# Second feed-forward on a residual divided by the norm's root, the final norm taking the root back in

## The chip, the cores and the metric

The kernel runs on one core of a Trainium2 chip. The metric is device microseconds (us) of one execution; the kernel before takes 1284.77 us, the median of 3 runs (1284.58 to 1285.41). Engines are named as in the profile: PE is TensorE (PEld its weight loads), DVE VectorE, ACT ScalarE, POOL GpSimd, SP SyncE. A name such as L736 is a line of the kernel's file.

## What is computed

One layer of a decoder trunk for 576 tokens (512 of a prompt and 64 of decode requests), 1024 wide: a first feed-forward, a mixer, a cross attention, a second feed-forward, and a last norm. Only its end matters here:

```python
h = h + cross_attend(rms_norm(h, g_cross), ...)
g, u = split(rms_norm(h, g_ffn2) @ w_ffn2_gu)      # 2816 columns each
h = h + 0.5 * (silu(g) * u) @ w_ffn2_down
y = rms_norm(h, g_final)        # x * rsqrt(mean(x*x) + EPS) * gain, per token
```

With R = rsqrt(mean(h*h) + EPS) of a token, g and u are the products of the weights with h times gain, each times that token's R.

## The kernel before

Tokens lie along the free dimension (576 columns, in two halves of 288), features on the 128 partitions; `h` is 8 chunks of 128x576. Every fp32 product is made of three reduced-precision (fp32r) matmuls: high by high, high by low, low by high. So each weight block has a high part (a rounding copy on ACT) and a low part (the difference, on DVE or POOL), and so have the activations.

Each engine has its own program, written out by hand in the order in which it runs; only semaphores tie the engines together. A wait holds back everything behind it on that engine. SP loads the weight blocks into `raw`, four buffers in turn.

The second feed-forward (from 877 to 1270 us) has three groups of columns: 8, 8 and 6 tiles of 128. A tile has a gate block and an up block. In the first group one tile is done plainly (`dense`, 48 matmuls for a block); the other 21 tiles are "units", in which gate and up of both token halves are four 2x2 block products done in seven (Strassen-Winograd): A11, A12, S1, S2, S4, A22, S3, with 12 matmuls each. After each group comes a down group: 8 blocks, each added to a chunk of `h`. Below, F is the first unit of the second feed-forward; F+1 to F+6 follow in the same group.

What each engine does for a unit v:

- PE, `unit(v)`: waits for the low part of A11 (`lo_a`, from POOL) and, in the first unit, until the plain gate is out of PSUM (`ps_free`); then the seven products. S2 of a unit waits until ACT has copied A11's product out (`e_ok`), S4 until ACT has copied S1's out.
- ACT, `unit(v)`: `high_last` (high parts of S3 and A22, L1562 and L1564), the copies out of PSUM (`keep`, L1583), the next unit's high parts (L1544, L1552), the gate's SiLU (L1602), and the high part of the hidden tile (L1607).
- DVE, `unit(v)`: the sums of weights for the next unit (L2118, L2121, L2125, L2128), low parts (L2134, L2139), `finish(v - 1)`, the low part of the hidden tile (L2179), and the gate's sum (L2206) and its product with R (L2208).
- `finish` makes the up tile `us` from two PSUM products (L2168), multiplies it by R (L2170) and by the SiLU (L2172). ACT's second copy out of PSUM in the next unit waits for L2168.
- POOL, `plain_lows`: for each unit the low part of A11 and A12 (L676) and of A22 (L679). Around it POOL adds the squares of `h` for the norms (`sums`, L519).

At the start of the second feed-forward ACT takes the logarithm and exponential of the mean square, and DVE refines R with one Newton step (`rms(3)`, L2069 to L2071). Then DVE evicts the plain gate (L2213), makes the low parts of F's sums (L2134) and one more sum (L2125), evicts the plain up block times R (L2217), and multiplies it by the SiLU (L2220).

At the end POOL has summed seven of eight chunks of squares in `acc`, PE makes the token means from `acc` and the last chunk, ACT takes the root (L1999), DVE inverts it (`inverse`, a reciprocal and a Newton step), and the transposed rows times gain are scaled by it on DVE and ACT and stored.

Of the kernel before, what the change touches and what calls it, by code (L numbers as in the profile page):

```python
# [9 lines left out]
ALU = mybir.AluOpType  # L10
ACT = mybir.ActivationFunctionType
# [4 lines left out]
KD = D // P  # L16
TP, NB, BT = 512, 8, 8
TS = NB * BT
T = TP + TS
TH = T // 2  # L20
NT = (T + P - 1) // P
# [3 lines left out]
EPS = 1e-6  # L25
# [26 lines left out]
def hymba_kernel(nc, A, O, consts):  # L52

    with ExitStack() as ctx:
# [10 lines left out]
        def S(name):  # L65
            if name not in sems:
                sems[name] = ctx.enter_context(nc.semaphore(name))
            return sems[name]


        cst = sb("cst", [P, C_END])
# [7 lines left out]
        eps = sb("eps", [P, 1])  # L79
# [22 lines left out]
        def view(base, at, *dims):  # L102
            n = 1
            for d in dims:
                n *= d
            v = base[:, at:at + n]
            if len(dims) == 1:
                return v
            names = "abcd"[:len(dims)]
            return v.rearrange(f"p ({' '.join(names)}) -> p {' '.join(names)}",  # L110
                               **{k: d for k, d in zip(names[1:], dims[1:])})
# [121 lines left out]
        def operand(v, j, low):  # L233

            if j >= A22:
                return (xl if low else xh)[:, 0:HK, TH + P * (j - A22):TH + P * (j - A22 + 1)]
            return view(ARr, 16 * T + 1024 * (5 * (v % 2) + j) + 512 * low, HK, P)

        def operands(v, j, n, low):

            return view(ARr, 16 * T + 1024 * (5 * (v % 2) + j), n, 1024)[:, :, 512 * low:512 * low + 512]

        yy = PR[:, 0:8, :]
        YB = (4, 6, 0, 2, 4)
# [256 lines left out]
        def _(e):  # L501
            e.memset(mean_d[:], 1.0 / D).then_inc(s_const, 1)
            e.memset(eps[:], EPS).then_inc(s_const, 1)
            e.memset(one[:], 1.0).then_inc(s_const, 1)
            e.memset(acc[:, T:], 0.0).then_inc(s_const, 1)
            e.memset(mst[:], 1.0).then_inc(s_const, 1)

            def sums(m):

                if m > 1:  # L510
                    e.wait_ge(acc_ready, 8 * (m - 1))
                e.wait_ge(ss, m)
                e.memset(acc[:, 0:T], 0.0).then_inc(acc_zero, 1)
                e.wait_ge(acc_zero, m)
                for k in range(KD - 1 if m == 4 else KD):
                    e.wait_ge(sq_ready, 8 * (m - 1) + k + 1)
                    if 8 * (m - 1) + k:
                        e.wait_ge(acc_ready, 8 * (m - 1) + k)
                    e.tensor_tensor(acc[:, 0:T], acc[:, 0:T], sq[:, k % 2, :], ALU.add).then_inc(acc_ready, 1)  # L519
# [117 lines left out]
            def s5_tables():  # L637
# [30 lines left out]
                        double()  # L668
                e.sem_inc(S("pool_points"), 1)

            def plain_lows(i):

                for v in range(FIRST_UNIT[i], FIRST_UNIT[i + 1]):
                    n = units[v]
                    e.wait_ge(S("hi_ok"), 4 * v + 1)
                    TTT(operands(v, A11, 2, 1), raw[:, n % 4, :].rearrange("p (s x) -> p s x", s=2),  # L676
                        operands(v, A11, 2, 0).bitcast(F32), ALU.subtract).then_inc(S("lo_a"), 1)
                    e.wait_ge(S("hi_ok"), 4 * v + 4)
                    TTT(operand(v, A22, 1), raw[:, (n + 1) % 4, 512:1024].rearrange("p (k n) -> p k n", k=HK),  # L679
                        operand(v, A22, 0).bitcast(F32), ALU.subtract).then_inc(S("lo_a"), 1)  # L680

            plain_lows(0)
            s5_chain()
# [40 lines left out]
            e.wait_ge(S("s_mm"), 4)  # L724
            e.memset(PTz, 0.0).then_inc(S("pool_points"), 1)
            sums(3)
            for i in range(2, 5):
                plain_lows(i)
            sums(4)
# [760 lines left out]
        def _(e):  # L1490
# [505 lines left out]
            for i in range(2, 5):  # L1996
                seven_group(i)
            e.wait_ge(ss, 5)
            e.activation(yst[:, 0, :], bank(1, NT), ACT.Sqrt, bias=eps[:]).then_inc(rt, 1)  # L1999
            e.wait_ge(S("yst_ok"), 1)  # L2000
            for m, j in enumerate(LEAVE):
                w = min(P, T - j * P)
# [7 lines left out]
        def _(e):  # L2010
# [3 lines left out]
            def own(ins):  # L2014
                mark(ins, "dve_own")
# [33 lines left out]
            def halves(b):  # L2049
                return PS[:, b:b + 2, 0:TH]  # L2050

            def two(ap):
                return ap.rearrange("p (a t) -> p a t", a=2)
# [6 lines left out]
                    STT(chunk(xl, k), chunk(h, k), gains[:, gain_of[m], bass.ds(k, 1)], chunk(xh, k).bitcast(F32),  # L2060
                        ALU.mult, ALU.subtract).then_inc(x_lo, 1)

            def inverse(root, square, tmp, name):

                own(e.reciprocal(root, root))
                newton(root, square, tmp, name)

            def newton(root, square, tmp, name):
                own(STT(tmp, root, -0.5, root, ALU.mult, ALU.mult))  # L2069
                own(STT(tmp, square, EPS, tmp, ALU.add, ALU.mult))  # L2070
                mark(STT(root, tmp, 1.5, root, ALU.add, ALU.mult), name)  # L2071

            def rms(m):
                if m == 0:
                    e.wait_ge(S("xsq_ok"), NT)
                    own(TSC(row_means, mst[:, 0:NT], 1.0 / D, None, ALU.mult))
                    e.wait_ge(rt, 1)
                    inverse(roots, row_means, row_tmp, "dve_own")
                    for j in range(NT):
                        w = min(P, T - j * P)  # L2080
                        TSC(xdiag[0:w, j * P:j * P + w], ident[0:w, 0:w], roots[0:w, j:j + 1], float(D), ALU.mult, ALU.mult).then_inc(S("xdiag_ok"), 1)
                    e.wait_ge(ss, 1)
                    mark(CP(R[:], bank(4, T)), "r_ready")
                    return
                if m == 3:
                    for j in (S1, S2, S4):
                        sum_of(j, FIRST_FFN2)
                e.wait_ge(rt, m + 1)
                newton(R[:], us[:] if m == 3 else bank(4, T), gs[:], "r_ready")

            def down(g):
                def body(i, n, par):
# [71 lines left out]
            def finish(v):  # L2164

                e.wait_ge(S("pr_done"), 7 * v + 7)
                e.wait_ge(S("e_ok"), 4 * v + 4)
                TTT(two(us[:]), two(sq[:, 1, :]), bank(u_bank(v), TH)[:, None, :].broadcast_to([P, 2, TH]), ALU.subtract).then_inc(S("c_ok"), 1)  # L2168
                e.wait_ge(S("c_ok"), 2 * v + 2)
                own(TTT(us[:], us[:], R[:], ALU.mult))  # L2170
                e.wait_ge(g_act, before(v) + 1)
                TTT(us[:], us[:], act[:], ALU.mult).then_inc(hid, 1)  # L2172

# [36 lines left out]
            def hidden(i, n, par, g):  # L2210

                if par == 0:
                    TTT(two(gs[:]), halves(6 if n == 2 else 0), two(R[:]), ALU.mult).then_inc(g_scaled, 1)  # L2213
                    e.wait_ge(g_scaled, i + (g["f0"] + 1))
                    e.sem_inc(ps_free, 1)
                else:
                    TTT(two(us[:]), halves(2), two(R[:]), ALU.mult).then_inc(ps_free, 1)  # L2217
                    e.wait_ge(ps_free, seq(n) + 3)
                    e.wait_ge(g_act, i + (g["f0"] + 1))
                    TTT(us[:], us[:], act[:], ALU.mult).then_inc(hid, 1)  # L2220
# [14 lines left out]
            def seven_group(i, within=None):  # L2235

                for v in range(FIRST_UNIT[i], FIRST_UNIT[i + 1]):
                    unit(v)
                finish(v)
                hidden_low(v)  # L2240
                g = groups[groups.index(seven_groups[i]) + 1]
                for b in range(KD):
                    n = g["n0"] + b
                    e.wait_ge(mm_done, seq(n) + 3)
                    STT(two(h[:, b, :]), halves(2 * (b % 2)), 0.5, two(h[:, b, :]), ALU.mult, ALU.add).then_inc(ps_free, 1)
                    if n == len(blocks) - 1:
                        e.wait_ge(ps_free, seq(n) + 3)
                        TSC(yy[:, b, :], h[:, b, :], gains[:, G_FINAL, b:b + 1], None, ALU.mult).then_inc(S("yy_v"), 1)
                    if b < KD - 2 or i in (1, 4):
                        conv(n + 2)  # L2250
                    if i in (0, 2, 3):
                        if b == KD - 3:
                            for j in (S1, S2, S3, S4):
                                sum_of(j, v + 1)
                        elif b == KD - 2:
                            low_sums(v + 1)
                    if i == 1 and b == 2:
                        second_half_low()
                    if within and b == 4:
                        within()  # L2260
                    elif within and b > 4:
                        matrix_step(2 * b - 10)
                        matrix_step(2 * b - 9)
# [509 lines left out]
            for i in range(2, 5):  # L2773
                seven_group(i)
            e.wait_ge(rt, 5)
            inverse(yst[:, 0, :], bank(1, NT), yst[:, 1, :], "yst_ok")
            for m, j in enumerate(LEAVE):
                w = min(P, T - j * P)
                e.wait_ge(S("y_tr"), m + 1)
# [48 lines left out]
```

## Time and profile before

| | before |
|---|---|
| time, median of 3 runs | 1284.77 us |
| span of the profiled execution (first to last instruction) | 1282.0 us |
| busy: PE, DVE, ACT, POOL | 1261.7, 857.1, 531.3, 353.9 us |
| granted TensorE clock, mean | 0.998 |
| the chain that ended last, on PE | 92% |

The profiled execution has no total of its own beside its span; the median of the timed runs is 2.77 us longer than that span, which is what lies around the first and the last instruction. A row of a timeline gives start, duration, engine, line, operation and operands, and in brackets the idle time of the engine before it and what ended that. Two matmuls that follow each other freely overlap in such rows, since the duration includes the drain of the pipeline.

### The profile page before, as it was taken

To read this page: it belongs to the slowest core of one execution; us is meant where nothing else is said; L and a number is where in the kernel's file an instruction comes from. 1 tells how busy PE (TensorE), PEld (TensorE's weight loads), DVE (VectorE), ACT (ScalarE), POOL (GpSimd) and SP (SyncE) were. 2 spreads that over 40 slices of the span, in tenths; PEclk is the share of its full clock that TensorE was granted. 3 is DMA by queue.
4 is the path that set the end of the run, shared out by engine and by line. 5 is a ranking of instruction groups with operands and counts; after the bars stand their busy time and mean duration, and the time that the engine had idled before them with its cause. 6 is when DMAs were issued, how large, how long until landed. Compare 5 with 4: busy or idle time off the path is not lost.

```text
span 1282.0 us, 24086 instructions
## 1 busy us (share of the span) xinstructions
PE 1261.7 (98%) x10151; PEld 1218.5 (95%) x10151; DVE 857.1 (67%) x1061; ACT 531.3 (41%) x803; POOL 353.9 (28%) x411
## 2 busy tenths in 40 slices
PE   7999999999999999999999999999999999999997
PEld 6999999999999999999899997599999999999997
DVE  4986479847885636558565437479995589637953
ACT  6644145511224422574443324246553255414543
POOL 0026723288893201000002100032330133102321
PEclk9999999999999999999999999999999999999999
DMA  6233323263223442125333756322332323323322
GB/s 182 81 96 90 91 85 99 83 137 91 74 65 94 91 81 65 51 69 154 119 89 93 232 197 223 122 83 66 100 99 83 99 83 99 91 83 91 87 63 74
DMA packets 221084, 129.94 MB, mean 101 GB/s; under 512 B 22256, under 2 KB 213280, under 8 KB 220960
## 3 DMA queue, kind: packets, MB, share of 16 engines
q1 hardware_dynamic: 217024, 123.83, 33.8%
q10 hardware_dynamic: 3952, 4.58, 1.1%
q8 instruction: 80, 1.31, 0.4%
q14 instruction: 28, 0.23, 0.1%
HBM read 121.42 MB, written 5.78 MB: 99 GB/s over the span
## 4 chain that ended last, share of the span: by engine, by line
PE 92%; DVE 4%; ACT 2%; issue 1%; DMA 1%; SPq 0%; ACTq 0%; DVEq 0%
PE PS L736 89%; PE PS L1361 1%; DMA AR<-in_x_prompt 1%; PE PS L806 0%; ACT wh L1500 0%; ACT gua L1649 0%; DVE Hs L2452 0%; DVE xl L2139 0%; PE PS L1338 0%; DVE AR L2780 0%; PE PS L953 0%; PE PS L1447 0%; DVE ARr L2134 0%; DVE yl L2233 0%; DVE wl L2027 0%
## 5 line engine op out<-in xcount | busy, mean ns | idle before, releaser
L1500 ACT ACTIVATE wh<-raw 128x1024 fp32r<-128x1024 f32 (+1 forms) x126 | 130.1, 1032 | 373.7 <-PE PS L736 373.1
L736 PE MATMUL PS<-yh,wh 128*128 128x288 f32 x960 | 205.6, 296 | 0.0
L736 PE MATMUL PS<-yl,wh 128*128 128x288 f32 x960 | 204.7, 295 | 0.0
L736 PE MATMUL PS<-yh,wl 128*128 128x288 f32 x960 | 204.6, 295 | 0.0
L2027 DVE TENSOR_TENSOR wl<-raw,wh 128x1024 fp32r<-128x1024 f32 (+1 forms) x126 | 154.9, 1229 | 63.7 <-ACT wh L1500 62.3
L736 PE MATMUL PS<-xh,ARr 128*128 128x288 f32 x792 | 174.1, 297 | 0.4 <-ACT sq L1583 0.2
L736 PE MATMUL PS<-xh,wh 128*128 128x288 f32 x736 | 164.4, 305 | 0.1
L736 PE MATMUL PS<-xh,wl 128*128 128x288 f32 x736 | 158.1, 297 | 0.0
L736 PE MATMUL PS<-xl,wh 128*128 128x288 f32 x736 | 157.9, 296 | 0.0
L736 PEld LDWEIGHTS PS<-yh,wh 128*128 128x128 f32 x960 | 154.1, 189 | 1.5 <-DVE yl L2705 0.8
L736 PEld LDWEIGHTS PS<-yh,wl 128*128 128x128 f32 x960 | 154.3, 189 | 0.0
L736 PEld LDWEIGHTS PS<-yl,wh 128*128 128x128 f32 x960 | 154.3, 189 | 0.0
L676 POOL TENSOR_TENSOR ARr<-raw,ARr 128x1024 fp32r<-128x1024 f32 x33 | 85.1, 2578 | 179.6 <-ACT ARr L1544 179.2
L736 PEld LDWEIGHTS PS<-xh,ARr 128*128 128x128 f32 x792 | 132.4, 188 | 1.1 <-ACT sq L1583 0.7
L519 POOL TENSOR_TENSOR acc<-acc,sq 128x576 f32<-128x576 f32 x31 | 52.6, 1697 | 276.9 <-issue 163.8
L736 PEld LDWEIGHTS PS<-xh,wh 128*128 128x128 f32 x736 | 118.3, 190 | 2.6 <-issue 1.1
L736 PEld LDWEIGHTS PS<-xh,wl 128*128 128x128 f32 x736 | 119.0, 190 | 0.0
L736 PEld LDWEIGHTS PS<-xl,wh 128*128 128x128 f32 x736 | 118.8, 190 | 0.0
L736 PE MATMUL PS<-xl,ARr 128*128 128x288 f32 x396 | 117.2, 296 | 0.0
L736 PE MATMUL PS<-ARr 128*128 128x288 f32 x792 | 114.5, 294 | 1.4 <-ACT sq L1583 1.4
L736 PEld LDWEIGHTS PS<-ARr 128*128 128x128 f32 x792 | 107.9, 188 | 1.6 <-issue 1.6
L1583 ACT ACTIVATE sq<-PS 128x288 f32<-128x288 f32 x132 | 54.1, 410 | 131.2 <-PE PS L736 83.3
(378 smaller groups left out, 2183.5 us busy)
## 6 DMA issues: line engine op xcount, KB each, us to landing
raw<-in_w_ffn_gu SPq DMA_DIRECT2D x88, 512.0 KB, 3.9
raw<-in_w_ffn_down SPq DMA_DIRECT2D x32, 512.0 KB, 3.9
raw<-in_w_in SPq DMA_DIRECT2D x16, 512.0 KB, 4.0
raw<-in_w_ckv SPq DMA_DIRECT2D x16, 512.0 KB, 3.8
raw<-in_w_ffn_down SPq DMA_DIRECT2D x16, 384.0 KB, 3.4
Hs<-in_cache_mem_k SPq DMA_DIRECT2D x6, 1024.0 KB, 6.5
raw<-in_w_out SPq DMA_DIRECT2D x8, 512.0 KB, 4.0
raw<-in_w_cq SPq DMA_DIRECT2D x8, 512.0 KB, 4.3
```

Source lines behind the costliest of these rows:

```text
L519: e.tensor_tensor(acc[:, 0:T], acc[:, 0:T], sq[:, k % 2, :], ALU.add).then_inc(acc_ready, 1)
L676: TTT(operands(v, A11, 2, 1), raw[:, n % 4, :].rearrange("p (s x) -> p s x", s=2), operands(v, A11, 2, 0).bitcast(F32), ALU.subtract).then ...
L736: return e.matmul(out, lhsT, rhs, start=start, stop=stop, **kw)
L1361: last = e.transpose(bank(4 + q % 3, P, at=f * M + j * P), KB[b][:, j, at:at + P], ident)
L1500: e.activation(wh[:, n % 2, 0:K * P], raw[:, n % 4, 0:K * P], ACT.Copy).then_inc(w_hi, 1)
L1583: e.activation(out, bank(b, TH), ACT.Copy, **kw).then_inc(S("e_ok"), 1)
L2027: TTT(wl[:, n % 2, 0:K * P], raw[:, n % 4, 0:K * P], wh[:, n % 2, 0:K * P].bitcast(F32), ALU.subtract).then_inc(w_lo, 1)
```

## The change

`h` is divided by R before the second feed-forward adds to it, so that the up tiles need not be multiplied by R: (h + 0.5 W(silu(g) u R)) / R = h/R + 0.5 W(silu(g) u). The gates still are multiplied. 1/R is (mean + EPS) times R; it is made by one more DVE operation in `rms(3)` and lies in `rinv`, in a constant's place that is free by then. POOL multiplies the eight chunks of `h` by it, between the low parts of the first group's units. The final norm of the new residual needs EPS/R^2 in the place of EPS: POOL starts the sum of squares with KD * EPS * rinv * rinv in the place of zero, and the last root and its Newton step add no EPS.

```diff
+        rinv = view(cst, C_SCAN, T)
...
-            e.memset(acc[:, T:], 0.0).then_inc(s_const, 1)
+            e.memset(acc[:, T:], 1.0).then_inc(s_const, 1)
...  POOL, sums(m)
-                e.memset(acc[:, 0:T], 0.0).then_inc(acc_zero, 1)
+                if m == 4:
+                    mul(acc[:, 0:T], rinv, rinv)
+                    e.tensor_scalar(acc[:, 0:T], acc[:, 0:T], KD * EPS, None, ALU.mult).then_inc(acc_zero, 1)
+                else:
+                    e.memset(acc[:, 0:T], 0.0).then_inc(acc_zero, 1)
...  POOL
+            def unscaled(k):
+                TTT(h[:, k, :], h[:, k, :], rinv, ALU.mult).then_inc(S("g_ok"), 1)
...  POOL, plain_lows(i), at the end of each unit v
+                    if i == 2:
+                        unscaled(v - FIRST_FFN2)
+                        if v == FIRST_FFN2 + 3:
+                            unscaled(KD - 1)
...  POOL, main order
             sums(3)
+            e.wait_ge(x_hi, 8 * 4)
+            e.wait_ge(x_lo, 8 * 4)
+            e.wait_ge(S("xg_ok"), 2 * HK)
+            e.wait_ge(S("t_sum"), 8 * HK)
+            e.wait_ge(S("rinv_ok"), 1)
             for i in range(2, 5):
                 plain_lows(i)
...  ACT, the last root
-            e.activation(yst[:, 0, :], bank(1, NT), ACT.Sqrt, bias=eps[:]).then_inc(rt, 1)
+            e.activation(yst[:, 0, :], bank(1, NT), ACT.Sqrt).then_inc(rt, 1)
...  DVE, rms(m)
                 newton(R[:], us[:] if m == 3 else bank(4, T), gs[:], "r_ready")
+                if m == 3:
+                    mark(STT(rinv, us[:], EPS, R[:], ALU.add, ALU.mult), "rinv_ok")
...  DVE, finish(v)
-                own(TTT(us[:], us[:], R[:], ALU.mult))
+                if v < FIRST_FFN2:
+                    own(TTT(us[:], us[:], R[:], ALU.mult))
...  DVE, hidden(): the plain up block
+                elif g is groups[FFN2]:
+                    e.wait_ge(g_act, i + (g["f0"] + 1))
+                    TTT(two(us[:]), halves(2), two(act[:]), ALU.mult).then_inc(hid, 1)
+                    e.wait_ge(hid, i + (g["f0"] + 1))
+                    e.sem_inc(ps_free, 1)
...  DVE, seven_group(i), before the down group
+                if i == 2:
+                    e.wait_ge(S("g_ok"), KD)
...  DVE, the last inverse
-            inverse(yst[:, 0, :], bank(1, NT), yst[:, 1, :], "yst_ok")
+            inverse(yst[:, 0, :], bank(1, NT), yst[:, 1, :], "yst_ok", 0.0)
```

## Rows read from the trace of the kernel before

**Rows 1.** The page: busy us of each engine, share of the span, instructions.
```profile
PE 1261.7 (98%) x10151; PEld 1218.5 (95%) x10151; DVE 857.1 (67%) x1061; ACT 531.3 (41%) x803; POOL 353.9 (28%) x411
```

**Rows 2.** Windows: stretch, length, busy us per engine, granted clock, DMA share, GB/s.
```profile
895.00:900.00 5.00, 3.62 (x28) 3.41 (x27) 4.93 (x7) 4.42 (x7) 2.56 (x2) 1.00 0.38 109
...
940.00:960.00 20.00, 20.00 (x153) 20.00 (x152) 18.96 (x22) 11.21 (x19) 8.23 (x4) 1.00 0.38 107
```

**Rows 3.** The chain that ended last, 855 to 935 us: start, length, what.
```profile
891.40 5.03 PE PS L736 x36
...
897.36 0.31 ACT sq L1583
...
910.46 0.42 ACT sq L1583
```

**Rows 4.** Timeline of PE, the first two units of the second feed-forward.
```profile
897.80 1.82 PE L736 MATMUL PS<-ARr 128*128 128x288 f32 x12 [1.38 <-ACT sq L1583]
...
905.82 1.74 PE L736 MATMUL PS<-ARr 128*128 128x288 f32 x12
907.40 0.30 PE L736 MATMUL PS<-xh,ARr 128*128 128x288 f32 x1
...
910.93 0.40 PE L736 MATMUL PS<-xh,ARr 128*128 128x288 f32 x1 [0.18 <-ACT sq L1583]
```

**Rows 5.** Waits, 1225 to 1240 us: who waited for whom, us, times, longest.
```profile
PEld PS L736 <- DVE yl L2179: 0.3, 1, 0.3
```

**Rows 6.** Timeline of DVE, from the last token sums to the second unit.
```profile
876.03 0.51 DVE L2159 SCALAR_TENSOR_TENSOR AR<-h,gains,AR 128x288 f32<-128x288 f32 x1
...
884.08 1.00 DVE L2159 SCALAR_TENSOR_TENSOR AR<-h,gains,AR 128x288 f32<-128x288 f32 x1
...
889.70 0.76 DVE L2071 SCALAR_TENSOR_TENSOR R<-gua,R 128x576 f32<-128x576 f32 x1
890.49 0.76 DVE L2213 TENSOR_TENSOR gua<-PS,R 128x576 f32<-128x576 f32 x1
...
898.83 2.80 DVE L2139 TENSOR_TENSOR xl<-AR,xh 128x512 fp32r<-128x512 f32 x1
...
904.72 0.76 DVE L2208 TENSOR_TENSOR gua<-gua,R 128x576 f32<-128x576 f32 x1
...
910.47 1.57 DVE L2170 TENSOR_TENSOR gua<-gua,R 128x576 f32<-128x576 f32 x1
```

**Rows 7.** Timeline of POOL, around the start of the second feed-forward.
```profile
880.47 1.43 POOL L519 TENSOR_TENSOR acc<-acc,sq 128x576 f32<-128x576 f32 x1 [4.98 <-ACT sq L1526]
881.86 2.91 POOL L676 TENSOR_TENSOR ARr<-raw,ARr 128x1024 fp32r<-128x1024 f32 x1
...
898.69 2.40 POOL L676 TENSOR_TENSOR ARr<-raw,ARr 128x1024 fp32r<-128x1024 f32 x1
907.32 1.30 POOL L679 TENSOR_TENSOR xl<-raw,xh 128x512 fp32r<-128x512 f32 x1 [6.23 <-ACT xh L1564]
```

**Rows 8.** Groups by line and form, DVE, 910 to 1235 us: busy, mean ns.
```profile
L2170 DVE TENSOR_TENSOR gua<-gua,R 128x576 f32<-128x576 f32 x21 | 28.5, 1357 | 0.7
...
L2139 DVE TENSOR_TENSOR xl<-AR,xh 128x512 fp32r<-128x512 f32 x19 | 13.2, 692 | 14.6 <-ACT xh L1562 14.6
```

**Rows 9.** Timeline of ACT, the third unit.
```profile
921.61 0.41 ACT L1583 ACTIVATE sq<-PS 128x288 f32<-128x288 f32 x1 [1.98 <-DVE gua L2168]
```

**Rows 10.** Timeline of DVE, evictions of the first and the second down group.
```profile
978.01 0.76 DVE L2245 SCALAR_TENSOR_TENSOR h<-PS,h 128x576 f32<-128x576 f32 x1 [2.32 <-PE PS L736]
...
984.25 0.76 DVE L2245 SCALAR_TENSOR_TENSOR h<-PS,h 128x576 f32<-128x576 f32 x1 [3.86 <-PE PS L736]
...
1117.10 0.76 DVE L2245 SCALAR_TENSOR_TENSOR h<-PS,h 128x576 f32<-128x576 f32 x1 [2.47 <-PE PS L736]
...
1123.50 0.76 DVE L2245 SCALAR_TENSOR_TENSOR h<-PS,h 128x576 f32<-128x576 f32 x1 [4.02 <-PE PS L736]
```

**Rows 11.** Timeline of POOL, before the last down group's squares.
```profile
1235.33 1.56 POOL L519 TENSOR_TENSOR acc<-acc,sq 128x576 f32<-128x576 f32 x1 [14.52 <-issue]
```

More of the change, by code:

```diff
@@ L2061, in norm_in, with inverse, newton @@
                         ALU.mult, ALU.subtract).then_inc(x_lo, 1)
-            def inverse(root, square, tmp, name):
+            def inverse(root, square, tmp, name, bias=EPS):
                 own(e.reciprocal(root, root))
-                newton(root, square, tmp, name)
-            def newton(root, square, tmp, name):
+                newton(root, square, tmp, name, bias)
+            def newton(root, square, tmp, name, bias=EPS):
                 own(STT(tmp, root, -0.5, root, ALU.mult, ALU.mult))
-                own(STT(tmp, square, EPS, tmp, ALU.add, ALU.mult))
+                own(STT(tmp, square, bias, tmp, ALU.add, ALU.mult))
                 mark(STT(root, tmp, 1.5, root, ALU.add, ALU.mult), name)
```

## The prediction, made before the change was run

> **What bounds the kernel now.** I read the page's busy times first: PE is busy 98% of the span, DVE 67%, POOL 28% [rows 1]. The change takes work from DVE, so the next question is where PE waits for DVE. Windows of the second feed-forward answer it for most of the stretch: between 940 and 960 us PE is busy for all 20.00 us although DVE is busy for 18.96 [rows 2]. DVE is nearly full there and still no bound. The chain of waits then shows where PE does stand still. From 891.40 us it runs three products (36 matmuls) of the first unit, F; ACT copies a product out from 897.36 to 897.67; PE goes on at 897.80 [rows 3, 4]. The timeline of PE calls that 1.38 us of idle time, and 0.18 us at 910.93, again behind ACT's copy [rows 4]. The third place is the entry to the last down group, 0.3 us behind the low part of the last hidden tile [rows 5]. The chain names no other PE stall between 911 us and the tail. So whatever DVE saves can return about 2 us here; the rest must fall into time in which DVE waits.
>
> True lost time is a little more than the idle time, because freely following products overlap: one that began at 905.82 and is listed with 1.74 us was followed at 907.40, not 907.56 [rows 4]. With 0.16 us added the first stall is 1.54 and the second 0.34 us. A product of 12 matmuls takes 1.6 us from start to start.
>
> **The change part by part.**
>
> *Twenty-one multiplications by R leave DVE.* L2170 is 28.5 us over 21 units, mean 1.36, but 0.76 where nothing holds it up [rows 8] (an operation of that shape, L2208, takes 0.76 [rows 6]). In the units they lie beside a PE that does not wait; I cost them at nothing, except at two places. At the second unit the copy that PE waits for does not depend on L2170, so nothing there. At the last down group it stands in the chain that PE waits for (difference, times R, times SiLU, high part, low part): taking 0.76 us out of a chain that is 0.3 us late removes the stall: -0.3 us. What is late next is the PE itself.
>
> *The plain up block* is evicted and multiplied by the SiLU in one operation instead of two: -0.79 on DVE with its gap. Its release of PSUM now waits for the SiLU, which ACT does while DVE makes two other operations (L2134, L2125) between gate and up block: nothing.
>
> *1/R is one more DVE operation* before the gate's eviction: +0.79 (as L2071, 0.76 and a gap [rows 6]). Together with the line above DVE's queue behind them is where it was.
>
> *POOL's low part of unit F moves behind 1/R.* This is the term that decides. Before, POOL did it as soon as the squares were added, from 881.86 on [rows 7], long before PE wanted it at 891.40. Now five waits stand ahead of `plain_lows(2)`, and the last of them is 1/R. Four are over earlier: the x parts and the token sums all come out ahead of R on DVE's queue. Two steps give the time. First, DVE is a little earlier: L2159 took 1.00 us instead of 0.51 while POOL's 2.91 us operation ran [rows 6, 7], and with that operation gone 0.49 us come back. R is then ready at 889.70 + 0.76 - 0.49 = 889.97 and 1/R at 890.76. Second, POOL starts 0.15 us later (PE began 0.15 us after the gate's eviction at 890.49 + 0.76 ended), takes 2.40 us where nothing blocks it [rows 7], and PE starts 0.15 us after that, at 893.45 instead of 891.40: +2.05 us. Everything queued on PE is behind that wait. Three products later S2 could start at 893.45 + 4.80 = 898.25. Before it started at 897.80, held by the copy that is now at the same place (DVE's queue to it neither grew nor shrank, or is up to 0.49 earlier). So the new wait swallows the old stall and adds 0.45 us. If DVE is not earlier (+0.49) and POOL's operation takes its blocked length of 2.91 (+0.51), it adds 1.45. The lower end is a POOL that costs nothing and a stall that goes by DVE's 0.49: -0.5.
>
> *POOL multiplies eight chunks by 1/R* in units F to F+6 (two in F+3). The nearest row is the addition of the same shape, 1.43 us [rows 7]; I take it. POOL has the room: 8.23 of 20 us in the steady stretch [rows 2], 1.43 more for each unit of 11.2 (84 matmuls). But POOL and DVE get into each other's way: L2139 took 2.80 us instead of 0.69 while POOL's operation of 898.69 to 901.09 ran, L2170 1.57 [rows 6 to 8]. The Trainium skill, page "SBUF — State Buffer", section "SBUF: two separate sides", makes this a lock on a shared port pair, held for a whole instruction by whichever started first, against DVE operations with two SBUF inputs. The trace agrees: L2139 ended 0.54 us after POOL's operation did.
>
> In unit F this is on the path. DVE's chain to the second stall is L2139, L2125, L2134, the gate's sum and L2208 (ending 905.48), then ACT's SiLU, and so on to the copy at 910.46 [rows 3, 6]. L2139 now meets the tail of the first scaling instead of the whole low part: 0.9 us less. L2125 behind it, free before, can meet the next unit's low part: up to 2.2 more. With 0.49 earlier from above that is between -1.4 and +0.8 us; S4 of F+1 could start, by PE alone, at 910.93 - 0.34 + 0.45 = 911.04, +0.11. So the end of this stretch moves by +0.11 to +0.8, and I take +0.5, as POOL will have been waiting when L2139 lets go. This replaces the +0.45 and is not added to it; with the upper end of the POOL wait it is +1.1 to +1.5.
>
> From F+2 on the margin is thin: the copy that S4 waits for ended at 922.02 [rows 9], and PE wanted it at 910.93 plus 84 matmuls of 0.133, 922.1. But PE is now 0.5 later and DVE has 1.57 less to do in each unit, against at most one scaling (1.43) to wait for. I cost this at nothing; the case in which it fails is the first rival. In F+3 POOL does 1.30 [rows 7] + 2 x 1.43 + 2.40 us and some blocked time, some 8 us, and the low part that it ends with is wanted about as late: nothing, or 0.3.
>
> *The wait of DVE for all eight scalings* stands before the first down eviction (978.01 [rows 10]); the last scaling comes at the head of F+6, most of a unit and a block of 6.24 us earlier: nothing.
>
> *POOL's new start of the sum* replaces one clearing by two operations; the first addition is at 1235.33, and POOL is idle for 14.52 us ahead of it [rows 11]. Two operations of even 2.40 us each fit: nothing on the path. The last root and Newton step have the same operations with other constants: nothing.
>
> The sum: +0.5 (start, both stalls included) - 0.3 (last group) = +0.2 us on a span of 1282.0, so 1282.2; the median is 2.77 us above the profiled span, and the forecast is 1285.0. Bounds of these terms: -0.5 - 0.34 - 0.3 = -1.1 below, +1.5 + 0.3 above: 1283.6 to 1286.6. What a measurement of this kernel can tell from no change is about 0.2%, 2.57 us; all of this is within.
>
> **The rivals.**
>
> 1. *POOL's scalings hold DVE up in each unit* (slower). Place: the units F+1 to F+6, whose copy had 0.1 us of margin. In a unit DVE's operations with two SBUF inputs can meet 5.1 us of POOL work (1.30 + 1.43 + 2.40) instead of 3.7. Decisive point: when the added waits exceed the 1.57 us that L2170 gave back and the 0.6 us of margin. If L2172 waits for a scaling (1.43) and L2179 or L2208 for the low part (2.40), the excess is 3.83 - 2.17, up to 1.7 us a unit, 10 us in six; at a third of that, 3.3 us, 1288.3. For it: the long L2139. Against: the removed operation was itself the one that met POOL. Chance 0.16.
>
> 2. *The matmuls fall into another rhythm.* The first down group's blocks follow each other every 6.24 us, the second's every 6.40 with the same DVE operations beside them [rows 10]: 48 matmuls at 130 or 133 ns. I know no cause. A moved start may change it: a group of eight blocks is worth 1.28 us, the last (six steps of weights) 0.96. If the first loses it, 1286.3; if the second and third gain it, 1282.8. Chance 0.15, both signs. The same skill page, section "Who interferes with whom", says that PE never waits on another engine's SBUF traffic. By that rule a lighter DVE cannot speed the matmuls; the two rhythms beside equal DVE work agree with it.
>
> 3. *The late POOL start costs nothing and the stalls shrink* (the lower bound): 1.1 us less than before, 1283.6. For it: DVE's 0.49. Against: 2.40 us of POOL cannot fit between 890.76 and 891.40. Chance 0.10.
>
> 4. *The units are bound by DVE after all*, and 0.76 us or more come back in each of 18 units: about -14, 1271. For it: 18.96 of 20 us busy. Against: PE has no gap there. Chance 0.04.
>
> **How the numbers follow.** Forecast 0.55, the rivals 0.16, 0.15, 0.10, 0.04. Faster by over 0.2% (below 1282.2): the last rival and 0.04 of the second at its low end, 0.08. Slower (above 1287.3): 0.13 of the first rival, and 0.05 for sums of the upper bound and a lost rhythm: 0.18. Same: 0.74. The range takes the forecast's bounds, and of the rhythms and the lock as much as leaves out 2 in 10: 1283.2 to 1287.4.
>
> **What would show it.** PE's first product of F starts near 893.4 instead of 891.40, released by POOL; no stall is left before S2 of F; a stall of a few tenths stays before S4 of F+1, and none in F+2 to F+6; PE's wait at the last down group is gone; DVE is about 28 us less busy and POOL about 14 more, with no other place that changes. PE stalls that repeat in each of F+1 to F+6 would make the prediction wrong on one side, a PE that is quicker in the units on the other.

## The result: 1287.8 us, 0.24% slower

| | before | after |
|---|---|---|
| time, median of 20 runs each | 1284.9 us | 1287.8 us (1286.04 to 1291.05) |
| ratio after to before, 95% interval | | 1.0024 (1.0019 to 1.0030) |
| span of the profiled execution | 1282.0 us | 1285.8 us |

1.0024 of 1284.9 is 3.1 us more (2.4 to 3.9). The forecast was 1285.0 with an upper end of 1287.4, so the time lies outside the range, on the side of rival 1.

Lines move with the edits. The matmul L736 is L755 now, POOL's low parts L676 and L679 are L686 and L689, DVE's `finish` is L2189 (difference) and L2194 (times SiLU). New are L679 (POOL's scaling of a chunk) and L2110 (1/R). The page's busy times of the kernel after, to be held against [rows 1]:

```profile
PE 1264.7 (98%) x10151; PEld 1220.5 (95%) x10151; DVE 851.3 (66%) x1040; ACT 531.3 (41%) x803; POOL 368.1 (29%) x420
```

POOL has 14.2 us more, as forecast. DVE has 5.8 us less, not 28: the first sign that something replaced what was removed. It is seen in DVE's groups by line and form, 910 to 1235 us before and 910 to 1238 us after (busy, mean ns). Before, first the operation that went and then the one behind it; after, the one that is left:

```profile
L2170 DVE TENSOR_TENSOR gua<-gua,R 128x576 f32<-128x576 f32 x21 | 28.5, 1357 | 0.7
L2172 DVE TENSOR_TENSOR gua<-gua 128x576 f32<-128x576 f32 x21 | 15.9, 758 | 0.7
```

```profile
L2194 DVE TENSOR_TENSOR gua<-gua 128x576 f32<-128x576 f32 x21 | 35.5, 1692 | 0.7
```

28.5 us of multiplications by R are gone, and 19.6 of them are back in the multiplication behind them. It takes 1.69 us now instead of 0.76. The first operation of `finish` with two SBUF inputs meets POOL's low part, whichever operation that is.

Where PE stands still is in its timeline (in brackets the idle time and its releaser; against [rows 4]):

```profile
894.29 0.40 PE L755 MATMUL PS<-xh,ARr 128*128 128x288 f32 x1 [2.15 <-POOL ARr L686]
912.67 0.40 PE L755 MATMUL PS<-xh,ARr 128*128 128x288 f32 x1 [0.62 <-ACT sq L1602]
924.39 0.40 PE L755 MATMUL PS<-xh,ARr 128*128 128x288 f32 x1 [0.30 <-ACT sq L1602]
...
936.12 0.40 PE L755 MATMUL PS<-xh,ARr 128*128 128x288 f32 x1 [0.33 <-ACT sq L1602]
959.15 0.40 PE L755 MATMUL PS<-xh,ARr 128*128 128x288 f32 x1 [0.32 <-ACT sq L1602]
...
970.87 0.40 PE L755 MATMUL PS<-xh,ARr 128*128 128x288 f32 x1 [0.32 <-ACT sq L1602]
```

The first row is the forecast wait for POOL, and S2 of F has no row of its own any more. 912.67 is S4 of F+1. The other four are S4 of F+2, F+3, F+5 and F+6, which did not wait before. From 912.67 to 924.39 and on to 936.12 are 11.72 and 11.73 us, where 84 matmuls of 0.133 need 11.17.

A bracket shows less than is lost, since matmuls that follow freely overlap. Below, "lost" is the sum of the start-to-start times of successive matmuls above 0.133 us, in three places:

| lost, us | F to S4 of F+1 | F+2 to F+6 | last down group | sum |
|---|---|---|---|---|
| before | 2.42 | 0 | 0.30 | 2.72 |
| after | 3.30 | 2.52 | 0 | 5.82 |

The difference is 3.1 us, the whole of the measured one. Of the 2.52, four units have 0.57 to 0.60 each and F+4 has 0.18. DVE and POOL show where they come from. First the kernel before in unit F+1, DVE and then POOL:

```profile
909.69 0.74 DVE L2168 TENSOR_TENSOR gua<-sq,PS 128x576 f32<-128x576 f32 x1
910.47 1.57 DVE L2170 TENSOR_TENSOR gua<-gua,R 128x576 f32<-128x576 f32 x1
912.07 0.76 DVE L2172 TENSOR_TENSOR gua<-gua 128x576 f32<-128x576 f32 x1
```

```profile
907.32 1.30 POOL L679 TENSOR_TENSOR xl<-raw,xh 128x512 fp32r<-128x512 f32 x1 [6.23 <-ACT xh L1564]
908.58 2.84 POOL L676 TENSOR_TENSOR ARr<-raw,ARr 128x1024 fp32r<-128x1024 f32 x1
```

Then the kernel after at the same place:

```profile
911.44 0.74 DVE L2189 TENSOR_TENSOR gua<-sq,PS 128x576 f32<-128x576 f32 x1
912.21 2.94 DVE L2194 TENSOR_TENSOR gua<-gua 128x576 f32<-128x576 f32 x1
```

```profile
909.06 1.30 POOL L689 TENSOR_TENSOR xl<-raw,xh 128x512 fp32r<-128x512 f32 x1 [5.51 <-ACT xh L1583]
910.32 1.87 POOL L679 TENSOR_TENSOR h<-h,cst 128x576 f32<-128x576 f32 x1
912.16 2.38 POOL L686 TENSOR_TENSOR ARr<-raw,ARr 128x1024 fp32r<-128x1024 f32 x1
```

Before, POOL's low part ended at 911.42; L2170 arrived 0.95 us ahead of that and ended 0.62 after it. From its start to the end of L2172 is 2.36 us. After, the scaling stands ahead of the low part. It ends as L2189 ends, POOL goes straight on, and L2194 arrives 0.05 us too late: it waits for the whole low part (912.16 + 2.38 = 914.54) and ends 0.61 us behind it. Its 2.94 us are 0.58 more than the two operations of before took together, and the loop over DVE, ACT's copy and PE had no slack, so PE loses those 0.58 in each such unit. Both chains start from ACT's high parts of the same unit, so the near miss repeats: L2194 takes 2.94 to 2.96 us in F+1, F+2, F+4 and F+5, and PE loses 0.57 to 0.60 us in the unit behind each. In F+3 two scalings stand ahead of the low part (3.27 us, up to 937.03), and L2194, arriving at 935.65, waits for the second of them instead: 1.99 us, and PE loses 0.18 in F+4.

The profiled spans differ by 3.8 us, not 3.1. The rest lies in code that the change doesn't touch (last section). Wherever a run's time and span are both known, the time is 1.75 to 1.86 us longer (1287.58 and 1285.8 for this profile). So, as an estimate, the profiled execution of before took 1283.8 us, about 1 us less than its median, and the 2.77 us of the section on time and profile before are not all outside the instructions.

### The profile page after: what moved, and what is told of

It reads as the page before. It is cut to its first block, busy times and chain, and to the rows that moved or that the text cites. A ratio compares the mean times of both kernels' runs of the same rounds, so it can differ in the third digit from the quotient of the medians.

```text
span 1285.8 us, 24079 instructions
## 1 busy us (share of the span) xinstructions
PE 1264.7 (98%) x10151; PEld 1220.5 (95%) x10151; DVE 851.3 (66%) x1040; ACT 531.3 (41%) x803; POOL 368.1 (29%) x420
## 4 chain that ended last, share of the span: by engine, by line
PE 89%; DVE 6%; issue 2%; ACT 2%; DMA 1%; SPq 0%; DVEq 0%; ACTq 0%
PE PS L755 85%; PE PS L1380 1%; DVE gua L2194 1%; DMA AR<-in_x_prompt 1%; ACT wh L1519 0%; DVE xl L2160 0%; DVE PS L2149 0%; DVE ARr L2155 0%; PE PS L1466 0%; PE PS L825 0%; DVE PS L2142 0%; DVE PS L2139 0%; ACT gua L1668 0%; DVE gua L2189 0%; DVE Hs L2481 0%
## 5 line engine op out<-in xcount | busy, mean ns | idle before, releaser
L755 PE MATMUL PS<-yh,wh 128*128 128x288 f32 x960 | 205.9, 296 | 0.0
L755 PE MATMUL PS<-yl,wh 128*128 128x288 f32 x960 | 205.0, 295 | 0.0
L755 PE MATMUL PS<-yh,wl 128*128 128x288 f32 x960 | 205.0, 295 | 0.0
L755 PE MATMUL PS<-xh,ARr 128*128 128x288 f32 x792 | 174.6, 297 | 4.1 <-POOL ARr L686 2.1
L755 PE MATMUL PS<-xh,wh 128*128 128x288 f32 x736 | 164.4, 305 | 0.1
L755 PE MATMUL PS<-xh,wl 128*128 128x288 f32 x736 | 157.8, 296 | 0.0
L755 PE MATMUL PS<-xl,wh 128*128 128x288 f32 x736 | 157.7, 296 | 0.0
L755 PEld LDWEIGHTS PS<-yh,wh 128*128 128x128 f32 x960 | 154.1, 188 | 1.3 <-DVE yl L2734 0.8
L755 PEld LDWEIGHTS PS<-yh,wl 128*128 128x128 f32 x960 | 154.4, 188 | 0.0
L755 PEld LDWEIGHTS PS<-yl,wh 128*128 128x128 f32 x960 | 154.4, 188 | 0.0
L755 PEld LDWEIGHTS PS<-xh,ARr 128*128 128x128 f32 x792 | 132.2, 188 | 5.9 <-ACT sq L1602 3.4
L686 POOL TENSOR_TENSOR ARr<-raw,ARr 128x1024 fp32r<-128x1024 f32 x33 | 82.4, 2496 | 189.1 <-ACT ARr L1563 179.7
L755 PEld LDWEIGHTS PS<-xh,wh 128*128 128x128 f32 x736 | 118.1, 190 | 2.6 <-issue 1.1
L755 PEld LDWEIGHTS PS<-xl,wh 128*128 128x128 f32 x736 | 118.8, 189 | 0.0
L755 PEld LDWEIGHTS PS<-xh,wl 128*128 128x128 f32 x736 | 118.7, 189 | 0.0
L755 PE MATMUL PS<-xl,ARr 128*128 128x288 f32 x396 | 117.0, 296 | 0.0
L755 PE MATMUL PS<-ARr 128*128 128x288 f32 x792 | 114.2, 294 | 0.0
L2274 DVE SCALAR_TENSOR_TENSOR h<-PS,h 128x576 f32<-128x576 f32 x40 | 30.2, 756 | 118.3 <-PE PS L755 118.3
```

Of the source, the lines that this page charges most:

```text
L755: return e.matmul(out, lhsT, rhs, start=start, stop=stop, **kw)
```

## The experiments

Theory A: the place of the scaling in POOL's order makes DVE wait a whole low part. Theory B: the late start of POOL (the wait for 1/R) sets a rhythm that makes the units late. Theory C: 1.43 us more of POOL's work costs this anywhere in the unit. "Lost" is as above; before it is 2.42, 0 and 0.30.

**no_scaling.** After, without POOL's eight scalings (so the residual is not divided and y is not the layer's):

```diff
-                    if i == 2:
-                        unscaled(v - FIRST_FFN2)
-                        if v == FIRST_FFN2 + 3:
-                            unscaled(KD - 1)
+                    if i == 2 and v == FIRST_FFN2:
+                        e.sem_inc(S("g_ok"), KD)
```

> The changed kernel without POOL's eight multiplications of h by 1/R; the residual is then not divided, so the outputs y are not the reference's; all else, the late start of POOL's first low part too, stays. Theory A (port lock): the up product L2194 meets POOL's low part only because a scaling stands ahead of that; without the scalings L2194 takes under 1.7 us in the units, PE has no stall of 0.3 us or more in the units F+2 to F+6, and the time is that of the kernel before within 0.5 us (start +0.44, second unit's stall at most +0.1, last down group -0.30). Theory B (late start): PE begins unit F 2 us late, DVE and ACT fall out of step with it and stay so; the stalls of 0.5 us in F+2 to F+6 remain and the time stays about 3 us above before.

1285.74 us, ratio 1.0006 (0.9998 to 1.0015); lost 3.93, 0, 0. The late start is still there (PE idle for 2.15 us behind POOL), and the stalls of the units are gone: B falls. DVE (here L2192 is the multiplication by the SiLU) and POOL in F+1:

```profile
909.57 0.74 DVE L2187 TENSOR_TENSOR gua<-sq,PS 128x576 f32<-128x576 f32 x1
910.34 1.67 DVE L2192 TENSOR_TENSOR gua<-gua 128x576 f32<-128x576 f32 x1
```

```profile
907.20 1.29 POOL L689 TENSOR_TENSOR xl<-raw,xh 128x512 fp32r<-128x512 f32 x1 [6.86 <-ACT xh L1581]
908.99 2.40 POOL L686 TENSOR_TENSOR ARr<-raw,ARr 128x1024 fp32r<-128x1024 f32 x1 [0.50 <-ACT ARr L1561]
```

The low part ends at 911.39 and DVE waits only for its rest, as L2170 did before. Of the 3.93 some 1.5 us are TensorE's clock (last section), not a wait. PE was late by that too, which could hide stalls here; scale_between, below, has the same late start at full clock and loses 0.17 us in F+2 to F+6.

**early_low.** The five waits stand behind the low parts of F and ahead of the first scaling, so POOL's first low part comes early again:

```diff
+                    if v == FIRST_FFN2:
+                        ready_to_scale()
...
             sums(3)
-            e.wait_ge(x_hi, 8 * 4)
...
-            e.wait_ge(S("rinv_ok"), 1)
```

> The changed kernel with the five waits moved from ahead of POOL's first low part of unit F to ahead of the first scaling, so that this low part is made early, as before the change. Theory A: PE starts unit F within 0.6 us of the gate's release again, S2 of F waits 1 to 1.5 us as before the change, but the stalls of about 0.57 us in F+1 to F+6 stay: 2 to 3 us above before. Theory B: with the late start gone the units run without stalls: 0 to 0.5 us below before.

1289.01 us, ratio 1.0032 (1.0021 to 1.0043); lost 3.79, 2.51, 0. POOL's low part of F starts at 884.11 and PE no longer waits for it, yet the entry loses no less: PE now waits 0.9 us at F for the gate's eviction (L2240), which stands behind 1/R (L2115) on DVE, 0.82 at S2 and 1.15 at S4 of F+1. DVE, and PE's first product of F, 0.15 us behind the end of that eviction:

```profile
892.74 0.76 DVE L2115 SCALAR_TENSOR_TENSOR cst<-gua,R 128x576 f32<-128x576 f32 x1
893.53 0.76 DVE L2240 TENSOR_TENSOR gua<-PS,R 128x576 f32<-128x576 f32 x1
```

```profile
894.44 0.37 PE L760 MATMUL PS<-xh,ARr 128*128 128x288 f32 x1 [0.91 <-issue]
```

The units lose what they lost. So taking the late start away saves nothing, neither at the entry nor behind it. The time is further above before than the 2 to 3 us expected, since PE loses more at the entry than was thought.

**scale_between.** The scaling goes between the low part of A11 and A12 and that of A22, the other side of the long operation; POOL does the same work:

```diff
+                    if i == 2 and v > FIRST_FFN2:
+                        unscaled(v - FIRST_FFN2 - 1)
                     e.wait_ge(S("hi_ok"), 4 * v + 4)
...              (low part of A22)
-                    if i == 2:
-                        unscaled(v - FIRST_FFN2)
...
+                    if i == 2 and v == FIRST_FFN2 + 6:
+                        unscaled(KD - 2)
+                        unscaled(KD - 1)
```

> The changed kernel with each scaling moved from behind the low part of A22 to ahead of it, where POOL is idle for 6 us in every unit (units F+1 to F+6; the last two scalings follow the last unit's low part). POOL does as much work as in the change. Theory A: it is the place in POOL's order that costs: L2194 under 1.7 us, no stalls of 0.3 us or more in F+2 to F+6, time within 0.6 us of before. Theory B: as long as the start is late the stalls stay, about 3 us above before. A third possibility, that POOL's added work costs wherever it stands: stalls of 0.3 us or more move to other DVE operations, 2 to 3 us above before.

1286.49 us, ratio 1.0006 (0.9997 to 1.0014); lost 3.31, 0.17, 0. This tells A from C: eight scalings in the same units, and the stalls are gone. DVE and POOL in F+1:

```profile
912.63 0.74 DVE L2190 TENSOR_TENSOR gua<-sq,PS 128x576 f32<-128x576 f32 x1
913.41 1.55 DVE L2195 TENSOR_TENSOR gua<-gua 128x576 f32<-128x576 f32 x1
```

```profile
910.26 1.30 POOL L691 TENSOR_TENSOR xl<-raw,xh 128x512 fp32r<-128x512 f32 x1 [5.51 <-ACT xh L1584]
911.51 2.83 POOL L686 TENSOR_TENSOR ARr<-raw,ARr 128x1024 fp32r<-128x1024 f32 x1
914.30 1.95 POOL L679 TENSOR_TENSOR h<-h,cst 128x576 f32<-128x576 f32 x1
```

The low part follows the A22 one at once, as before; DVE waits for its last 0.93 us, and then the scaling waits for DVE (1.95 us instead of 1.43), where nobody waits for it.

**idle_scaling.** The kernel before with a multiplication of the same shape on POOL at the change's places (its product is read by nobody); as in the change, DVE waits for all eight before the down group:

```diff
+                    if i == 2:
+                        if v == FIRST_FFN2:
+                            e.wait_ge(r_ready, 4)
+                        idle_scaling(v - FIRST_FFN2)
+                        if v == FIRST_FFN2 + 3:
+                            idle_scaling(KD - 1)
```

> The kernel before with one part of the change alone: POOL multiplies the chunks of h by R into a place that nothing reads, at the very points where the change scales h, with the two multiplications in F+3; DVE keeps L2170, POOL's first low part stays early. Theory A: now L2170 meets POOL's whole low part (2.9 us instead of 1.58), DVE's loop grows by about 1.3 us in each unit and PE waits about 1.2 us in each of four to six units: 5 to 7 us above before, twice what the change costs, since there L2170's own 0.76 us are saved. Theory B: nothing, within 0.5 us of before, as the start is not late.

1293.37 us, ratio 1.0063 (1.0050 to 1.0076), 8.1 us more; lost 3.54, 5.93, 0.30. The added work costs without the rest of the change, and more than with it. The expectation had the size nearly right and the wrong operation. DVE and POOL in F+1:

```profile
912.87 0.76 DVE L2180 TENSOR_TENSOR gua<-gua,R 128x576 f32<-128x576 f32 x1
913.66 2.84 DVE L2182 TENSOR_TENSOR gua<-gua 128x576 f32<-128x576 f32 x1
```

```profile
910.98 1.87 POOL L673 TENSOR_TENSOR cst<-h,R 128x576 f32<-128x576 f32 x1
912.93 2.95 POOL L680 TENSOR_TENSOR ARr<-raw,ARr 128x1024 fp32r<-128x1024 f32 x1
```

Here DVE won the race by 0.06 us: the multiplication by R ran at 912.87, the low part waited for it (2.95 us instead of 2.38), and then POOL went ahead of the next DVE operation. One difference from the change is enough to decide this: here POOL waits until its product is done, and the low part starts 0.08 us behind that product's end at 912.85; in the change it starts 0.03 us ahead of the scaling's end. L2180 and L2182 take 3.63 us from start to end, 1.27 more than the 2.36 of before; PE loses 1.25 to 1.28 in each unit of F+2 to F+6 but one (0.86). Three kernels, one sum: 2.36 us of `finish` is free, 2.94 costs 0.58, 3.63 costs 1.27. Losing the race or winning it costs a whole low part either way; what helps is that the low part begins well before DVE comes (1.89 us in the kernel before, 1.35 in no_scaling).

**both_moved** joins early_low and scale_between.

> The changed kernel with POOL's first low part early again and each scaling ahead of the low part of A22 (the two edits tried singly before). Theory A (each POOL operation that DVE meets on the way to the copy that PE waits for costs its rest): no stalls in F+2 to F+6; in F and F+1 the entry stalls stay near 3.3 us together, since 1/R still stands in DVE's chain and L2139 or L2125 still meets POOL; about +0.3 to +1.0 us against before. If the late start were the cost at F+1, the entry would fall to 2 us and the time to 0.7 us under before.

1285.12 us, ratio 1.0006 (0.9997 to 1.0015); lost 3.86, 0.17, 0. The units are cured, the entry is not.

**scale_in_down.** Early low parts as in early_low; all eight scalings behind the last low part of the group, one wait in DVE for each down block:

```diff
+            plain_lows(2)
+            ready_to_scale()
+            for k in range(KD):
+                unscaled(k)
-            for i in range(2, 5):
+            for i in range(3, 5):
                 plain_lows(i)
...  DVE, for b in range(KD) of the down group
+                    if i == 2:
+                        e.wait_ge(S("g_ok"), b + 1)
```

> The changed kernel with all eight scalings after the last unit of the first group, where POOL is idle for 50 us and DVE has little to do; each down block's eviction waits for its own chunk. POOL's first low part is early again. Theory A: the units lose nothing; PE's lost time from 890 to 1235 us is 2.2 to 2.7 us instead of 2.72 before and 5.83 in the change, the stall at the last down group is gone, the time is 0 to 0.7 us below before. Theory C (POOL's eight operations cost wherever they stand): they now hold up the down group's evictions or PE's first block, 1 us or more above before.

1286.55 us, ratio 1.0009 (1.0000 to 1.0018); lost 2.65, 1.13, 0. A new stall of 0.87 us stands at the down group's entry, which the expectation missed. PE, then DVE ahead of it, then POOL:

```profile
973.39 0.53 PE L758 MATMUL PS<-yh,wh 128*128 128x288 f32 x2 [0.70 <-DVE gua L2231]
```

```profile
968.56 2.21 DVE L2049 TENSOR_TENSOR wl<-raw,wh 128x1024 fp32r<-128x1024 f32 x1 [0.17 <-ACT wh L1522]
970.69 1.98 DVE L2204 TENSOR_TENSOR yl<-gua,yh 128x576 fp32r<-128x576 f32 x1
972.60 0.74 DVE L2231 TENSOR_TENSOR gua<-sq,PS 128x576 f32<-128x576 f32 x1
```

```profile
963.95 15.70 POOL L679 TENSOR_TENSOR h<-h,cst 128x576 f32<-128x576 f32 x8
```

Eight scalings in a row take 1.96 us each, and DVE's operations take turns with them: 2.21 and 1.98 us where they take 1.23 and 0.75 without (next run). So the scalings cost here too, where DVE's work is on the path.

**late_reciprocal.** As scale_in_down, and 1/R is a reciprocal on DVE behind the last hidden tile's low part, so neither the start of F nor that tile sees any of it:

```diff
-                if m == 3:
-                    mark(STT(rinv, us[:], EPS, R[:], ALU.add, ALU.mult), "rinv_ok")
...
                 hidden_low(v)
+                if i == 2:
+                    e.reciprocal(rinv, R[:]).then_inc(S("rinv_ok"), 1)
```

> As the kernel with the scalings in the down group, and 1/R is no longer made by an operation ahead of the plain gate's eviction but by a reciprocal of R after the last hidden tile of the first group. If 1/R in DVE's entry chain is what keeps the rest of the entry stall, PE's first product of F starts within 0.45 us of the end of the plain blocks, S2 of F waits about 0.75 us (1.54 before), S4 of F+1 at most 0.45; lost time 1.4 to 1.9 us instead of 2.72: 0.8 to 1.4 us below before. If the chain to S2 does not go through it, as scale_in_down. The reciprocal of 576 columns may take 3 to 4 us and then delays the first eviction by as much, within the block of 6.2 us: no PE stall from it.

1284.68 us, ratio 0.9997 (0.9988 to 1.0005); lost 1.87, 0, 0. DVE and POOL at the group's end:

```profile
967.17 1.23 DVE L2049 TENSOR_TENSOR wl<-raw,wh 128x1024 fp32r<-128x1024 f32 x1 [0.63 <-ACT wh L1522]
968.31 0.75 DVE L2202 TENSOR_TENSOR yl<-gua,yh 128x576 fp32r<-128x576 f32 x1
...
974.99 3.75 DVE L2270 RECIPROCAL cst<-R 128x576 f32<-128x576 f32 x1
980.36 0.76 DVE L2277 SCALAR_TENSOR_TENSOR h<-PS,h 128x576 f32<-128x576 f32 x1 [1.63 <-POOL h L679]
```

```profile
978.90 13.11 POOL L679 TENSOR_TENSOR h<-h,cst 128x576 f32<-128x576 f32 x8 [15.50 <-DVE cst L2270]
```

The first eviction waits 1.63 us for POOL, and PE loses nothing there. What this version saves is the stall at the last down group and part of S2's: 0.85 us less lost than before, which is 0.07% and cannot be told from no change. It is the only version that loses less than the kernel before; in time it equals it.

**change_again.** The change itself, profiled a second time.

> The changed kernel unchanged, for a second profile. Theory A: the same stalls (2.3 us ahead of F, 0.8 to 0.9 at F+1, 0.57 in F+2, F+3, F+5 and F+6, 0.2 in F+4). The rhythm of the down groups (6.24 or 6.40 us a block) is no property of the kernel: at least one of the two first-group rhythms may differ from the first profile's, as may a fall of the granted clock after the 2.3 us gap.

One execution, 1289.82 us; lost 3.94, 1.97, 0. Some 1.5 of the 3.94 is the clock again; PE then comes late enough that S4 of F+1 and of F+2 need not wait, and the later units stall as in the first profile. The sum of 5.91 is that of the first profile, 5.82.

The lost time, against before's 2.72, lies inside the interval of the timed difference in every kernel (us). The interval of scale_between doesn't reach that of after; those of no_scaling, scale_between, both_moved and late_reciprocal include no change:

| | lost more | timed, from the ratio |
|---|---|---|
| after | +3.1 | +3.1 (2.4 to 3.9) |
| no_scaling | +1.2 | +0.8 (-0.3 to 1.9) |
| early_low | +3.6 | +4.1 (2.7 to 5.5) |
| scale_between | +0.8 | +0.8 (-0.4 to 1.8) |
| idle_scaling | +7.0 | +8.1 (6.4 to 9.8) |
| both_moved | +1.3 | +0.8 (-0.4 to 1.9) |
| scale_in_down | +1.1 | +1.2 (0 to 2.3) |
| late_reciprocal | -0.9 | -0.4 (-1.5 to 0.6) |

## Why the prediction was wrong

*Right.* The start: +0.44 us of lost time up to S2 for the forecast +0.45, by the mechanism named. POOL's low part of F starts behind 1/R, takes 2.37 us, and PE waits 2.15 us for it; no wait is left before S2. DVE and POOL at that place, against [rows 6, 7]:

```profile
890.06 0.76 DVE L2090 SCALAR_TENSOR_TENSOR R<-gua,R 128x576 f32<-128x576 f32 x1
890.86 0.76 DVE L2110 SCALAR_TENSOR_TENSOR cst<-gua,R 128x576 f32<-128x576 f32 x1
```

```profile
891.87 2.37 POOL L686 TENSOR_TENSOR ARr<-raw,ARr 128x1024 fp32r<-128x1024 f32 x1 [9.11 <-DVE cst L2110]
```

The last down group: -0.30 for -0.3. The plain up block, the wait for all scalings and POOL's new start of the sum (1.15 and 2.24 us, then 11.51 idle) cost nothing, as said.

*A little off.* The entry as a whole was put at +0.5, and S4 of F+1 brought another +0.44 on top of the +0.44 of the start, together +0.88. That is inside what the text gave for the two waits at their worst, and by the operation that it named: L2125, L2146 now, was free before and met the next unit's low part.

```profile
901.32 2.78 DVE L2146 TENSOR_TENSOR AR<-raw 128x512 f32<-128x512 f32 x1
```

In scale_in_down, without a scaling in F, PE idles 0.17 us at S4 of F+1, about as before; in early_low, which has the same early low part and the scaling in F, 1.15.

*Wrong.* The step that failed is "From F+2 on the margin is thin ... DVE has 1.57 less to do in each unit, against at most one scaling (1.43) to wait for. I cost this at nothing". It cost 2.52 us. Three readings are wrong in it. First, 1.57 us was L2170's duration, and 0.81 of that was its wait for POOL's low part. Such a wait does not go with the operation; the next one with two SBUF inputs inherits it. Only 0.76 was there to be given back, as no_scaling shows: L2192 takes 1.67 and not 0.76. The last 15 units, which have no scaling, say the same: DVE's groups from 972 to 1235 us, before and after,

```profile
L2170 DVE TENSOR_TENSOR gua<-gua,R 128x576 f32<-128x576 f32 x15 | 19.8, 1321 | 0.5
L2172 DVE TENSOR_TENSOR gua<-gua 128x576 f32<-128x576 f32 x15 | 11.4, 758 | 0.5
```

```profile
L2194 DVE TENSOR_TENSOR gua<-gua 128x576 f32<-128x576 f32 x15 | 20.5, 1369 | 0.5
```

Second, the scaling was priced by its own 1.43 us as the longest wait. Its place ahead of the low part moves the low part by 1.43 us and more, and what DVE met there was not a scaling but the start of the low part: 2.33 us of waiting instead of 0.95. The price of an operation put into POOL's queue is where it shifts those behind it. The forecast for the 28 us of DVE fell with the first reading.

Third, "PE is now 0.5 later" was counted as margin. PE was 0.88 later, and yet the 0.58 us that DVE's chain grew by were lost in full: S4 of F+1 had itself waited for that chain, so PE and DVE were late together. Lateness that doesn't come from that chain does give margin: in change_again the lower clock made PE 1.5 us late, and S4 of F+1 and F+2 did not wait.

Rival 1 had the place, the condition (that the waits exceed what L2170 gave back and the margin) and the low part as a thing waited for. It added two waits in a unit, L2172 for a scaling and L2179 or L2208 for the low part, up to 1.7 us. One was there, L2172 (L2194 now) for the low part, and it cost 0.58 us in four units and 0.18 in one. That its own "a third" of ten (3.3 us) is close to 2.5 is luck. It was given 0.16, because "the removed operation was itself the one that met POOL"; that argument is the first wrong reading again.

The Trainium skill, page "SBUF — State Buffer", section "SBUF: two separate sides", says that the shared port pair goes to whichever of the two engines' operations starts first, for the whole instruction. The traces agree where the units show such a wait: each of these DVE operations ends 0.54 to 0.62 us after POOL's, and a POOL operation that comes second is longer by its wait (2.95 us for 2.38). Read with care that rule gives the result: a lock held for a whole instruction is paid by arrival time, and 0.05 us decided over 2.4.

## What to carry to other kernels

When an operation whose duration contains a wait for a shared port is removed, count only its free duration as saved; the wait moves to the next operation that needs the port. When work is put on the other engine of that port, don't price it by its length but redraw the order of both queues: the long operation that it pushes back is what the first engine will meet, and in a loop without slack the near miss is paid in every turn. Try the new operation on either side of the long one before the whole idea is judged.

## What else the runs showed of the hardware

*TensorE's clock after the wait for POOL.* In the change's first profile PE waited 2.15 us and went on at full clock. In change_again and no_scaling it waited the same 2.15 us and fell to its lower level, 1.2 GHz: the same matmuls followed each other every 240 ns. Windows of after and then of change_again (length, busy us of PE, PEld, DVE, ACT and POOL, granted clock):

```profile
894.20:898.50 4.30, 4.21 (x31) 4.21 (x32) 4.12 (x7) 2.37 (x5) 0.49 (x2) 1.00 0.45 126
```

```profile
896.00:899.40 3.40, 3.40 (x17) 3.40 (x16) 3.22 (x5) 2.38 (x5) 0.46 (x1) 0.52 0.52 153
```

It costs about 14 times 0.107 us, 1.5 us. In change_again nearly all of it was given back, since the units behind it stall less (5.91 us lost in all, 5.82 in the first profile). In scale_between PE waited 2.15 us as well and kept its clock, and so it did before behind the 1.38 us at S2. What decides between the executions was not tried.

*Two rhythms.* The first feed-forward's first down group, which the change doesn't touch, evicts a block every 6.24 us in the profile of before and every 6.40 us after:

```profile
129.94 0.76 DVE L2245 SCALAR_TENSOR_TENSOR h<-PS,h 128x576 f32<-128x576 f32 x1 [3.86 <-PE PS L736]
136.18 0.76 DVE L2245 SCALAR_TENSOR_TENSOR h<-PS,h 128x576 f32<-128x576 f32 x1 [3.86 <-PE PS L736]
```

```profile
129.81 0.76 DVE L2274 SCALAR_TENSOR_TENSOR h<-PS,h 128x576 f32<-128x576 f32 x1 [4.02 <-PE PS L755]
136.21 0.76 DVE L2274 SCALAR_TENSOR_TENSOR h<-PS,h 128x576 f32<-128x576 f32 x1 [3.99 <-PE PS L755]
```

These are the 130 and 133 ns matmuls of [rows 10]. The second feed-forward's first down group has 6.24 in the first profile of the change and 6.40 in change_again, the same kernel. So rival 2's rhythm, 1.28 us for eight blocks, differs between executions of one kernel, and two profiles can differ by it where the kernels don't. Of the ten profiles five have 6.24 in that group and five 6.40. Whether the change makes one of them more frequent is not shown, and the cause stays open.
